# Strassen's products in both layers' gate/up and down projections, the conditioning sums moved to layer 0 and the weight sums to GpSimd

## The reference, cut to what matters

```python
D_FF = 2816                                   # 11 blocks of 256 hidden columns, 22 tiles of 128
h = rms_norm(x, ffn_norm[l])                  # (256, 1024)
gate, up = jnp.split(h @ w_gate_up[l], 2, axis=-1)
x = x + (jax.nn.silu(gate) * up) @ w_down[l]  # l = 0, 1

mod = jax.nn.silu(c) @ ada_w + ada_b          # second block: (1024) @ (1024, 6144)
sh1, sc1, g1, sh2, sc2, g2 = jnp.split(mod, 6, axis=-1)
```

## Time and profile before

| | us |
|---|---|
| three runs | 1870.46, 1870.53, 1870.74 (median 1870.53) |
| the profiled execution, its own time | 1870.68 |
| its span, first to last instruction | 1868.6 |
| feed-forward of layer 0, from block 1 to the last down product | 182.9 to 383.5 |
| feed-forward of layer 1, the same | 555.8 to 780.0 |

### The profile page before, as it was taken

One profiled execution on the slowest core, in us unless ns is written; L12 is line 12 of the kernel. 1 busy time (PEld: TensorE's weight loads), 2 busy tenths in 40 slices (PEclk: granted clock), 3 DMA queues, 4 the chain that ended last, 5 costly groups with the idle time before them and its releaser, 6 DMA issues.

```text
span 1868.6 us, 23771 instructions
## 1 busy us (share of the span) xinstructions
PE 1820.7 (97%) x8690; PEld 926.1 (50%) x8691; DVE 732.7 (39%) x1501; ACT 244.4 (13%) x506; POOL 207.3 (11%) x399
## 2 busy tenths in 40 slices
PE   9999999999999999999999999999999999999997
PEld 4466878744667777565433333333333333333332
DVE  4554453445536763297522122212222212222222
ACT  1411101114110000232101010101000101000101
POOL 0200000002006868422000000000000000000000
PEclk9999999999999999999999999999999999999999
DMA  8142443341448874316799999999999699999995
GB/s 323 68 180 98 180 181 136 113 193 68 180 191 319 325 287 185 130 46 268 284 424 427 428 429 428 429 429 428 429 429 428 252 425 428 429 427 429 428 427 240
DMA packets 41184, 558.13 MB, mean 299 GB/s; under 512 B 4599, under 2 KB 5495, under 8 KB 6557
## 3 DMA queue, kind: packets, MB, share of 16 engines
q1 hardware_dynamic: 40396, 556.06, 72.0%
q10 hardware_dynamic: 720, 1.18, 0.2%
HBM read 556.16 MB, written 1.06 MB: 298 GB/s over the span
## 4 chain that ended last, share of the span: by engine, by line
PE 68%; DMA 22%; DVE 7%; ACT 1%; issue 1%; DVEq 0%; SPq 0%; ACTq 0%; POOLq 0%
DMA mega<-in_exp_w 17%; PE PS L2270 12%; PE PS L1955 9%; PE PS L1977 8%; PE PS L2310 8%; PE PS L1639 7%; PE PS L1904 7%; DMA tenth<-in_exp_w 5%; PE PS L1816 3%; PE PS L2256 2%; PE PS L2154 1%; PE PS L2000 1%; PE PS L1994 1%; PE PS L2263 1%; PE PS L1610 1%
## 5 line engine op out<-in xcount | busy, mean ns | idle before, releaser
L2270 PE MATMUL PS<-mega,tb 128*64 128x512 f32 x1728 | 378.2, 593 | 9.0 <-POOLq L2434 8.2
L2270 PEld LDWEIGHTS PS<-mega,tb 128*64 128x64 f32 x1728 | 123.5, 137 | 258.3 <-issue 239.9
L1526 DVE TENSOR_SCALAR tmp<-PS 128x512 f32<-128x512 f32 x34 | 23.5, 692 | 557.1 <-PE PS L2270 557.1
L2310 PE MATMUL PS<-mega,tb 128*64 128x512 f32 x896 | 198.4, 595 | 0.0
L1639 PE MATMUL PS<-mega,hT 128*128 128x512 f32 (+2 forms) x416 | 171.1, 551 | 0.0
L1955 PE MATMUL PS<-hT,mega 128*128 128x256 f32 x736 | 161.0, 379 | 0.0
L1977 PE MATMUL PS<-mega,late 128*128 128x512 f32 x352 | 154.7, 593 | 0.0
L1955 PEld LDWEIGHTS PS<-hT,mega 128*128 128x128 f32 x736 | 139.5, 190 | 22.6 <-issue 4.3
L2310 PEld LDWEIGHTS PS<-mega,tb 128*64 128x64 f32 x896 | 61.9, 137 | 133.1 <-issue 128.0
L1639 PEld LDWEIGHTS PS<-mega,hT 128*128 128x128 f32 x416 | 74.6, 190 | 59.1 <-issue 47.0
L1977 PEld LDWEIGHTS PS<-mega,late 128*128 128x128 f32 x352 | 65.8, 190 | 75.8 <-issue 75.6
(11 more groups left out here) (496 smaller groups left out, 2026.9 us busy)
## 6 DMA issues: line engine op xcount, KB each, us to landing
mega<-in_exp_w SPq DMA_DIRECT2D x154, 2048.0 KB, 26.4
mega<-in_w_gate_up SPq DMA_DIRECT2D x22, 2048.0 KB, 9.0
tenth<-in_exp_w SPq DMA_DIRECT2D x19, 2048.0 KB, 29.3
late<-in_exp_w SPq DMA_DIRECT2D x19, 2048.0 KB, 28.4
mega<-in_ada_w SPq DMA_DIRECT2D x12, 2048.0 KB, 9.6
mega<-in_w_down SPq DMA_DIRECT2D x10, 2048.0 KB, 7.3
mega<-in_w_in_part SPq DMA_DIRECT2D x9, 2048.0 KB, 10.0
mega<-in_w_out SPq DMA_DIRECT2D x6, 2048.0 KB, 8.5
```

What stands on the lines that cost most here:

```text
L1526: ch.to(v.tensor_scalar(mgs, PS[:, 0, :], SWIGLU_LIMIT, None, ALU.min), g.m_gs, n + 1)
L2270: ins = pe.matmul(PS[64 * h:64 * h + 64, b, :], xg[:, o:o + 64], slot_of(r, s)[:, w:w + 512], start=False, stop=k == KC - 1, skip_group_ch ...
L2310: ins = pe.matmul(PS[64 * h:64 * h + 64, 2, :], aT[:, P * (c % 4) + 64 * (c // 4):P * (c % 4) + 64 * (c // 4) + 64], slot_of(r, s)[:, o:o ...
```

## The change

What it does, part by part:

- Both layers do block 0 plainly and blocks 1 to 10 by seven products. Banks alternate (0 to 2 and 3 to 5), so a block may start when the block before the last is activated.
- The down projection is a second stage after all eleven blocks, in six slots of four tiles (the last of two). Each slot is seven products of (2 x) two tiles, accumulated over the slots in seven PSUM banks, 77 matmuls of 128x512 in a layer. It needs four sums of activations (VectorE, `act_sums`) and four of weights in each slot.
- The weight sums of layer 0, 15 times four of 128x1024 and once four of 128x512, are made by GpSimd, released by FIFTH and FOURTH of the block before; those of layer 1 stay on VectorE, put between its other steps.
- The conditioning's twelve halves are loaded in layer 0, one beside each gate/up block, and summed by VectorE at the head of blocks 1 to 10 and of down slots 0 and 1. TensorE sums each over partitions after the block (`summed(h)`, bank 7).
- `params` is loaded in both layers; the gates' factor `g_row` is made by GpSimd, 2048 wide, in layer 1. The S5 work of VectorE in layer 1 moves to blocks 2 to 5, so GpSimd's tables can start after block 3.
- At a layer's end `summed_up` combines the seven banks into `x` by ten sums of 128x512.

The core of the diff:

```diff
+DOWN_ORDER = [(FIRST, SECOND, FOURTH, SIXTH, FIFTH, THIRD, SEVENTH)] + [(FIRST, SECOND, SIXTH, FIFTH, FOURTH, THIRD, SEVENTH)] * (DN_SLOTS - 2) + [
+    (FIRST, SIXTH, SECOND, FIFTH, THIRD, SEVENTH, FOURTH)]
+def first_plan():
+    blocks = [("gu", i) for i in range(FF_BLOCKS)] + [("dn", j) for j in range(DN_SLOTS)]
+    keys = blocks[:2] + [("params", 0), ("ada", 0), ("ada", 1)] + blocks[2:5]
+    for h in range(2, HALVES):
+        keys += [("ada", h), blocks[h + 3]]
+    return keys + blocks[HALVES + 3:]
...
 (VectorE)
                 def fast_block(i):
-                    n = l * (FF_BLOCKS - 1) + i - 1
+                    n, q = fast_before(l, i), 3 * (i % 2)
+                    if l == 0 and i >= 3:
+                        half_taken(i - 3)
+                    condition(i, range(KC))
                     v.wait_ge(g.e_e, 3 * n + 2)
                     link(v.tensor_tensor(p16, e1, e6, ALU.add))
+                    if l == 1:
+                        v.wait_ge(g.p_p, 7 * n + FIFTH)
+                    next_sums(i, (1,))
                     v.wait_ge(g.p_p, 7 * n + SEVENTH)
-                    link.to(v.tensor_tensor(p167, PS[:, 6, 0:256], e1, ALU.add), g.s_v, n + 1)
+                    link.to(v.tensor_tensor(p167, PS[:, q + 2, 0:256], e1, ALU.add), g.s_v, n + 1)
+                    next_sums(i, (2,))
...
-                    if i + 1 < FF_BLOCKS:
-                        weight_sums(i + 1, (1, 3))
+                def down_slot(j):
+                    if j + 1 < DN_SLOTS:
+                        if j >= 1:
+                            v.wait_ge(g.p_v, products_of(l, j))
+                        act_sums(j + 1)
+                    if l == 0 and FF_BLOCKS + j - 3 < HALVES:
+                        half_taken(FF_BLOCKS + j - 3)
+                    condition(FF_BLOCKS + j, range(KC))
...
+                def summed_up(done, between):
+                    v.wait_ge(g.s_re, 2 * l + 2)
+                    link(v.tensor_tensor(x00, x00, r1, ALU.add))
+                    link(v.tensor_tensor(r1, r1, product(SIXTH), ALU.add))
+                    link(v.tensor_tensor(x00, x00, product(SECOND), ALU.add))
+                    link(v.tensor_tensor(r2, r1, product(FIFTH), ALU.add))
+                    link(v.tensor_tensor(x01, x01, r2, ALU.add))
+                    done(0, v.tensor_tensor(x01, x01, product(THIRD), ALU.add))
+                    link(v.tensor_tensor(r1, r1, product(SEVENTH), ALU.add))
+                    link(v.tensor_tensor(x10, x10, r1, ALU.add))
+                    link(v.tensor_tensor(x11, x11, r1, ALU.add))
+                    between()
+                    link(v.tensor_tensor(x11, x11, product(FIFTH), ALU.add))
+                    done(1, v.tensor_tensor(x10, x10, product(FOURTH), ALU.add))
...
 (TensorE)
                     if i >= 2:
-                        pe.wait_ge(g.s_actv, l * FF_BLOCKS + i)
+                        pe.wait_ge(g.s_actv, l * FF_BLOCKS + i - 1)
...
-                    pe.wait_ge(g.t_w, 4 * n + 4)
+                    pe.wait_ge(g.t_w, m + 4)
                     pe.wait_ge(g.s_v, n + 1)
-                    product(a22, wsum4, 6, False)
+                    product(a22, s4, q + 2, False)
...
+                first_block()
+                for i in range(1, FF_BLOCKS):
+                    fast_block(i)
+                    if l == 0 and i >= 2:
                         summed(i - 2)
+                for j in range(DN_SLOTS):
+                    down_slot(j)
+                    if l == 0 and FF_BLOCKS - 2 + j < HALVES:
+                        summed(FF_BLOCKS - 2 + j)
...
 (GpSimd)
+                if l == 0:
+                    pool.wait_ge(g.s_wo, TT)
+                    for u in range(1, FF_BLOCKS + DN_SLOTS):
...
+                        pool.wait_ge(landed[slot], 16 * use + 16)
+                        if 2 <= u <= FF_BLOCKS:
+                            pool.wait_ge(g.p_p, 7 * fast_before(0, u - 1) + FIFTH)
...
+                        link.to(pool.tensor_tensor(s1, b12, b11, ALU.subtract), g.t_w, m + 1)
+                        link.to(pool.tensor_tensor(s2, b22, s1, ALU.subtract), g.t_w, m + 2)
+                        link.to(pool.tensor_tensor(b12, b22, b12, ALU.subtract), g.t_w, m + 3)
+                        if 2 <= u <= FF_BLOCKS:
+                            pool.wait_ge(g.p_p, 7 * fast_before(0, u - 1) + FOURTH)
...
+                        link.to(pool.tensor_tensor(s4, b21, s2, ALU.subtract), g.t_w, m + 4)
+            pool.wait_ge(g.d_ev, HALVES)
+            pool.wait_ge(g.r_row, 32)
+            link.to(pool.tensor_tensor(g_row, gate_rows, post, ALU.mult), g.s_gd, 1)
             pool.wait_ge(g.dve2, DVE2["u_cs"] + 1)
```

More of the change, by code:

```diff
@@ L181, in place_loads @@
-    for n, (key, l) in enumerate(LOADS):
+    place, done, turn = {}, [0] * RING, 0
+    for key, l in LOADS:
         kind, i = key
-        if kind in ("params", "glu"):
+        if kind in ("params", "glu") or (key, l) == (("dn", DN_SLOTS - 1), 1):
             continue
-        if n < len(LAYER_LOADS):
-            slot = n % LAYER_RING
+        if kind == "ada":
+            slot = 4 + i % 2
         elif key in LAST_SLOT:
             slot = LAST_SLOT[key]
-        elif kind == "gu":
-            slot = 1 + i % 2
+        elif l == 1 and kind in ("gu", "dn"):
+            slot = (1, 2, 0)[(i + (FF_BLOCKS if kind == "dn" else 0)) % 3]
@@ L191, in place_loads @@
         else:
-            slot = 0 if kind == "dn" else 4 + i % 2
+            slot, turn = turn % LAYER_RING, turn + 1
         place[key, l] = (slot, done[slot])
@@ L1170, in weight_sums @@
                     if 1 in which:
[L1171 to L1174 removed]
+                        link.to(v.tensor_tensor(s1, b12, b11, ALU.subtract), g.t_w, n + 1)
+                    if 2 in which:
+                        link.to(v.tensor_tensor(s2, b22, s1, ALU.subtract), g.t_w, n + 2)
@@ new lines, in next_sums, with act_sums @@
+                def next_sums(i, which):
+                    if l == 0:
+                        return
+                    if i + 1 < FF_BLOCKS:
+                        gate_sums(i + 1, which)
+                    else:
+                        down_sums(0, which)
+                def act_sums(j):
+                    n = 4 * (DN_SLOTS * l + j)
+                    a11, a12, a21, a22 = (act_tiles(j, l, t, h) for t in range(TT) for h in range(2))
+                    s1, s2, s3, s4 = (act_sum(j, i) for i in range(4))
+                    link.to(v.tensor_tensor(s1, a21, a22, ALU.add), g.s_s, n + 1)
+                    link.to(v.tensor_tensor(s2, s1, a11, ALU.subtract), g.s_s, n + 2)
+                    link.to(v.tensor_tensor(s4, a12, s2, ALU.subtract), g.s_s, n + 3)
+                    link.to(v.tensor_tensor(s3, a11, a21, ALU.subtract), g.s_s, n + 4)
```

566 lines of the change are left out of this document (311 added, 255 removed).

## The result

The changed kernel takes **1949.6 us** (median of 4 runs, 1949.0 to 1952.0), the kernel before 1870.6 beside it: ratio **1.0423** (95% interval 1.0405 to 1.0441). Forecast was 1927.7 with a range of 1886 to 1948: the direction is right, the size is 22 us too low. The profiled execution's span is 1946.9 us against 1868.6, so 78.3 us are to be found; the forecast had 57.0.

The account below looks back on a forecast made before the run. GpSimd's sums holding VectorE were to set layer 0's pace, about 18.9 us a block, TensorE idling before FOURTH. Terms 59.3 + 2.1 + 3.1 - 29.5 + 14 + 8 = +57.0 on 1870.7 gave 1927.7 us, range 1886 to 1948.

Parts of the forecast that it names:

- the hold: Layer 0 blocks: each 2.37 us GpSimd sum keeps VectorE off for 2.04; three before p16 add 6.1 us.
- The fourth sum: Layer 0 blocks: starting at the last block's FOURTH, it holds VectorE's 256-wide product, +1.2 us.
- The page of the Trainium skill that was weighed: Says the later instruction is blocked for the other's whole length: each hold 2.37, total about 1940 us.
- blocks and clock together: Layer 0, blocks 1 to 10 with the summation behind block 10, clock included: 196.2 us.
- The clock term: Layer 0: 5.5 us waits lower TensorE's clock, FOURTH costs 0.9 more in each of nine blocks: +8 us (0 to 16).
- the down stage: Layer 0's down slots: GpSimd has slack and VectorE's activation sums are a slot ahead, so slots cost their products.
- Any wait in the down slots: Listed sign that the forecast is wrong; down slots were expected to take 12.03 us.
- the start of block 1: Layer 0: GpSimd's first four sums run beside VectorE's row squares and root, making the root late: +3.0 us.
- the upper case of 4.3: Ahead of block 1: the root's delay is 4.3 us if the row squares are held too.
- layer 1: Cheaper blocks and moved conditioning save 33.0 us, GpSimd's g_row and beside work cost 3.5: -29.5 us.
- layer 1's end and the tables: First tile's root stands behind five adds, +3.1 us; GpSimd's tables end 46 us after the last product, +14.
- case (4): Rival: clock falls at every wait and tables come 30 us late, 1952 us; chance 0.09.

Follow-up runs that it names:

- e7_all: First combined kernel, from the changed kernel: PSUM accumulation, reordered VectorE steps, later first and fourth GpSimd sums, angles and cosines one block earlier; 1887.3 us, ratio 1.0069.
- e1_narrow: Changed kernel with GpSimd's layer 0 weight sums cut to 16 columns of one plane, so its numbers are not the reference's; 2014.9 us, ratio 1.0764.
- e14_best2: Third combined kernel: the second (1875.3 us) plus shortened tables, g_row's product in four pieces, and VectorE's output matrices in two parts; 1862.3 us, ratio 0.9948.
- e6b_early: Changed kernel with layer 1's angles, sines and cosines one block earlier, so GpSimd's tables start earlier; 1944.9 us, ratio 1.0393.
- e10_best: Second combined kernel, from the changed kernel: PSUM accumulation, reordered VectorE steps, re-timed GpSimd sums and g_row, angles and cosines one block earlier; 1875.3 us, ratio 1.0016.
- e2_psum: Changed kernel with the conditioning halves of blocks 1 to 10 accumulating in PSUM bank 6, only the last step writing SBUF; 1889.9 us, ratio 1.0100.
- e12_halved: Changed kernel with each of GpSimd's layer 0 weight sums split into two instructions of 128x512, same data; 1929.2 us, ratio 1.0309.
- e5_start: Changed kernel with GpSimd's first four sums released by the root's diagonal instead of the attention's last products; 1954.4 us, ratio 1.0426.

## Why the prediction was right and wrong, step by step

**Right in kind and size: the hold.** In the block above seven held and unheld L877 take 11.56 against 5.48 us (the seven at 420.58, below, stand beside no sum): 6.08 for three holds, 2.03 each, forecast 2.04 and 6.1. The fourth sum cost 1.27, forecast 1.2. The experiments show the mechanism: 82 us go with the sums' width, 60 with one operand's place. The page of the Trainium skill that was weighed (SBUF — State Buffer, Who interferes with whom) is confirmed for instructions with two SBUF inputs; its "whole instruction" is about 0.35 us longer than the holds at both lengths measured.

**Right in the sum, in part by luck: blocks and clock together.** 199.7 us against 188.2 + 8. From one summation behind a block to the next it is 20.4 to 21.3 us in the six blocks in which FOURTH waits 5 us, more than the 19.8 forecast (18.9 and 0.9 of clock), and about 17 in two: there the slow clock before delayed FIFTH, the three sums came later and caught p16 and us1, of which the second is not on FOURTH's path. Nobody had forecast the short blocks; without them the stretch would be some 8 us longer (an estimate from these spacings). The clock term was 8, the runs give 10 net.

**Wrong: the down stage** ("in the down stage GpSimd has slack ... so the slots cost their products"), 9.4 of the 22 us. VectorE's timeline in slots 0 and 1, then TensorE's summation:

```profile
396.11 15.61 DVE L877 SCALAR_TENSOR_TENSOR tmp<-mega,st,tmp 128x512 f32<-128x512 f32 x7
411.88 2.33 DVE L1258 TENSOR_TENSOR mega<-tenth 128x256 f32<-128x256 f32 x1 [0.16 <-DVE tmp L877]
414.24 2.45 DVE L1259 TENSOR_TENSOR mega<-mega,tenth 128x256 f32<-128x256 f32 x1
416.72 2.45 DVE L1260 TENSOR_TENSOR mega<-tenth,mega 128x256 f32<-128x256 f32 x1
...
420.58 5.48 DVE L877 SCALAR_TENSOR_TENSOR tmp<-mega,st,tmp 128x512 f32<-128x512 f32 x7
...
420.17 2.05 PE L1693 MATMUL PS<-tmp,K 128*128 128x512 f32 x2 [6.36 <-DVE st L899]
422.00 5.29 PE L2078 MATMUL PS<-mega,tenth 128*128 128x512 f32 x8
```

The slack was worked out for TensorE's need of the sums, not for what they do to VectorE. Eight sums run almost without a gap from 397.6 to 418.9, hold five L877 and three activation sums (2.33 to 2.45 instead of 0.43), and behind those stands the taken half for which TensorE's next summation waits: 6.36 us, and 2.7 of low clock after it. In `e7_all`, with the taken half ahead of the activation sums, this wait is gone, and in `e1_narrow`, with the order unchanged and GpSimd's sums tiny, it is gone too and the slots cost their products (68.9 us). "Any wait in the down slots" had been named as a sign of being wrong.

**Wrong by half: the start of block 1**, 6.0 instead of 3.0. VectorE's second row square and first step of the root, before and after the change, and TensorE's diagonal:

```profile
170.33 1.22 DVE L807 CUSTOM_DVE_ANT_0 mega<-x 128x1024 f32<-128x1024 f32 x1
...
171.59 0.17 DVE L803 TENSOR_SCALAR st<-st 128x2 f32<-128x2 f32 x1
...
171.60 3.25 DVE L853 CUSTOM_DVE_ANT_0 mega<-x 128x1024 f32<-128x1024 f32 x1
...
174.89 2.18 DVE L849 TENSOR_SCALAR st<-st 128x2 f32<-128x2 f32 x1
...
179.94 1.22 PE L2028 MATMUL PS<-tmp,K 128*128 128x128 f32 x4 [4.19 <-DVE tmp L1204]
180.95 8.11 PE L2022 MATMUL PS<-hT,mega 128*128 128x256 f32 x32
```

Both squares were held (2.27 and 3.25 instead of 1.22), and the root's first step by 2.0, so the diagonal comes at 179.94, 4.6 later, near the upper case of 4.3 that was named; what was left out is that TensorE's 4.19 us wait lowers its clock for the 32 instructions after it (8.11 instead of 7.07). The forecast took the clock only in the blocks.

**Right: layer 1**, -29.8 for -29.5. TensorE waits there twice, 1.22 in block 1 and 1.34 in block 6, where 2.5 and 1 were forecast; the other blocks are unhindered.

**Half right: layer 1's end and the tables.** TensorE's transposes; GpSimd's tables 0 and 1 and its next step; VectorE's wait for it.

```profile
845.03 1.97 PE L2129 MATMUL PS<-K,mega 128*128 128x128 f32 x8 [8.62 <-ACT mega L677]
...
684.86 0.10 POOL L2533 MEMSET mega<- 128x4 f32 x1 [45.91 <-DVE late L920]
...
739.78 0.10 POOL L2533 MEMSET mega<- 128x4 f32 x1
...
887.40 2.34 POOL L2578 TENSOR_TENSOR mega<-mega 128x1024 f32<-128x1024 f32 x1
...
892.26 2.29 DVE L1421 TENSOR_TENSOR mega<-mega 128x2048 f32<-128x2048 f32 x1 [14.42 <-POOL mega L2579]
```

A table takes 54.9 (forecast 54). The first began at 684.86, 42.8 us behind block 1's start, the last ended at 886.2, 50 after the last product (forecast 46), and VectorE waits 14.42 for GpSimd, as forecast. The price by the stages is 16.1, and the run with short tables takes 14.4 of it away; the forecast was 14. The transposes' wait of 8.62 was forecast as 5.4. It is 5.3 in the runs where GpSimd was idle (`e14_best2`) or in a table's narrow instructions (`e6b_early`, `e10_best`) during the ten adds and the root. Beside a table's wide instructions, here, the adds of 0.69 are 1.08 and 1.63 and steps of 0.22 are 0.89 and 1.11. So holds are the 3.2 us there as well. But the tables' end is not a place that can be moved freely: 12.5 us earlier gave 7, because the last table then ran through VectorE's busiest stretch. There GpSimd's 512-wide instructions take 1.90 to 3.13 instead of 1.04 to 1.27, and VectorE's own row gets 5 us longer and becomes the limit (`e10_best`).

**The range.** The measured time is 1.6 us above its end at 1948; without the down stage's 9.4 us it would have lain inside. The end was set by a case (4) that put the whole excess on clock and tables. With the down stage bounded from above by the holds that can fall into it, as the blocks were, the upper end is some 10 us higher.

**Open.** Why the two-part half gained 19 and not 45: its two loops were seen, not followed through all ten blocks. Which VectorE instructions with one SBUF input are held: only L849 and its like were seen, in passing, and no run was made for them. Layer 0 as it was before with only layer 1 changed was not tried.

## To carry to other kernels

A wide elementwise instruction given to GpSimd is paid by VectorE wherever VectorE reads two operands from SBUF, and at times where it reads one; count holds per loop and per stage, also in the stages whose own engines have slack. An accumulator in an unused PSUM bank frees the VectorE chain that uses it entirely (60 of the 82 us here); where there is no bank, cut GpSimd's instructions small and release them where VectorE's instructions have a PSUM input. Where TensorE waits a few microseconds, add the low clock after it to the wait, in every stage.

## What the runs showed of the hardware

- The hold is GpSimd's length less 0.34 to 0.4 us at 2.37 and at 1.27 us, and strikes a 0.16 us VectorE instruction as it does a 0.75 us one (L900: 2.30). A VectorE instruction that starts while GpSimd's is under way is held for the rest of it only: us1 (2.00) in `e2_psum` ends 0.28 us behind GpSimd's sum. In turn a tiny GpSimd instruction waits for VectorE (0.57 instead of 0.20 in `e6b_early`); a table takes 55 us beside VectorE's work and 36 nearly alone.
- One input in SBUF is no safeguard for a `tensor_scalar`: L849 of 128x2 takes 2.18 beside GpSimd's 128x1024 sums, 1.11 beside 128x512 ones (`e12_halved`) and 0.17 alone (`e5_start`). A `scalar_tensor_tensor` with one input in SBUF and one in PSUM was not held in any block of `e2_psum`.
- Halving GpSimd's instructions at equal data took 20 us off the kernel.
- TensorE's clock: waits of 0.5 and 1.2 us left the products behind them at full speed; one of 1.95 lowered it (5.44 for 32 instructions), one of 2.12 left it once (3.81 for 32, `e14_best2`) and lowered it once (3.59 for 16 instead of 2.02, `e7_all`), and the 2.35 of the earlier trace rows left it, so the length of a wait alone doesn't tell; after a 5.2 us wait sixteen instructions took 3.75 instead of 2.02, and the summation behind them was often slow, too.
- scalar_tensor_tensor of 128x512 takes 0.75 us with the accumulator in SBUF or in PSUM alike; tensor_scalar of 128x512 0.75 into PSUM and 0.49 into SBUF.
